# Expert stage of a hybrid decoder layer: token rows gathered as quarter rows and turned by VectorE in 32x32 blocks instead of by TensorE

## The reference

```python
order = jnp.argsort(flat_e)                       # flat_e: expert of each (token, choice) pair, 4096 of them
padded = ((counts + 127) // 128) * 128            # each expert's rows padded to blocks of 128
rows = jnp.zeros((n_rows, 1024)).at[dest].set(h[stok])          # token rows, gathered by expert

def expert_block(args):                           # xb 128 x 1024, e the expert of the block
    xb, e = args
    hid = jax.nn.silu(xb @ w_gate[e]) * (xb @ w_up[e])          # 1024 x 512 each
    return hid @ w_down[e]                                      # 512 x 1024

out = lax.map(expert_block, (rows.reshape(n_blocks, 128, -1), block_e))
return segment_sum(out[dest] * gate, stok)        # added to x, then a last RMSNorm
```

## Time and profile before

| | us |
|---|---|
| median of 3 runs | 2213.04 (2211.13 to 2219.3) |
| the profiled execution | 2212.72 |
| its span | 2211.1 |
| expert loop, first gate product of the loop to the last | about 1261 to 2138 |
| PE busy | 1996.7 (90%) |
| DVE busy | 1415.3 (64%) |
| ACT busy | 1072.4 (49%) |
| POOL busy | 525.4 (24%) |

### The profile page before, as it was taken

The page is one execution under the profiler, slowest core; times in us unless marked ns, Lnnn a source line. Parts: engine busy times, 40 slices in busy tenths (PEclk is TensorE's granted clock), DMA queues, the critical chain, the costliest instruction groups (busy, mean ns, idle before and its releaser), DMA issues. The chain is left out here.

```text
span 2211.1 us, 32053 instructions
## 1 busy us (share of the span) xinstructions
PE 1996.7 (90%) x10153; PEld 1672.5 (76%) x10154; DVE 1415.3 (64%) x2368; ACT 1072.4 (49%) x1591; POOL 525.4 (24%) x637
## 2 busy tenths in 40 slices
PE   6999999886898988969996699999999999999970
PEld 5887888785687878858885588888888888888860
DVE  4675687466797887945556675675568755546344
ACT  4322211224377787753223364665567655545433
POOL 2000111241000000000000254454445545344430
PEclk9999999998899999989997699999999999999995
DMA  8675986835435323024335588797889978667637
GB/s 263 218 228 196 327 288 223 262 133 124 123 69 125 76 69 67 1 84 167 134 134 200 196 309 281 255 331 273 283 277 387 348 268 304 188 229 238 218 85 314
DMA packets 170121, 458.37 MB, mean 207 GB/s; under 512 B 19872, under 2 KB 69104, under 8 KB 144432
## 3 DMA queue, kind: packets, MB, share of 16 engines
q1 hardware_dynamic: 122896, 285.30, 37.4%
q0 software_dynamic: 31008, 138.37, 20.5%
q10 hardware_dynamic: 16128, 33.56, 4.3%
HBM read 342.08 MB, written 115.10 MB: 207 GB/s over the span
## 5 line engine op out<-in xcount | busy, mean ns | idle before, releaser
L2215 DVE TENSOR_TENSOR w_down_lo<-w_down_raw,w_down_hi 128x2048 fp32r<-128x2048 f32 x64 | 144.1, 2289 | 124.5 <-ACT w_down_hi L2152 123.0
L2299 PE MATMUL m_bank<-w_down_hi,hidden_T_hi 128*128 128x512 f32 x392 | 160.4, 409 | 6.8 <-DVE w_down_lo L2215 6.8
L2215 DVE TENSOR_TENSOR w_gate_lo<-w_gate_raw,w_gate_hi 128x2048 fp32r<-128x2048 f32 x63 | 141.6, 2289 | 38.8 <-ACT w_gate_hi L2152 32.4
L2278 PE MATMUL m_bank<-w_gate_hi,rows_T_hi 128*128 128x512 f32 x392 | 156.5, 399 | 6.4 <-DVE rows_T_lo L2220 3.9
L2278 PE MATMUL m_bank<-w_up_hi,rows_T_hi 128*128 128x512 f32 x392 | 158.8, 405 | 0.0
L2279 PE MATMUL m_bank<-w_gate_lo,rows_T_hi 128*128 128x512 f32 x392 | 156.1, 398 | 0.0
L2280 PE MATMUL m_bank<-w_gate_hi,rows_T_lo 128*128 128x512 f32 x392 | 156.0, 398 | 0.0
L2215 DVE TENSOR_TENSOR w_up_lo<-w_up_raw,w_up_hi 128x2048 fp32r<-128x2048 f32 x64 | 146.2, 2287 | 15.1 <-ACT w_up_hi L2152 15.1
L2300 PE MATMUL m_bank<-w_down_lo,hidden_T_hi 128*128 128x512 f32 x392 | 155.4, 396 | 0.0
L2280 PE MATMUL m_bank<-w_up_hi,rows_T_lo 128*128 128x512 f32 x392 | 154.8, 395 | 0.0
L2279 PE MATMUL m_bank<-w_up_lo,rows_T_hi 128*128 128x512 f32 x392 | 154.5, 394 | 0.0
(11 more groups left out here) (424 smaller groups left out, 5288.3 us busy)
## 6 DMA issues: line engine op xcount, KB each, us to landing
w_gate_raw<-in_w_gate_dram SPq DMA_DIRECT2D x64, 1024.0 KB
w_down_raw<-in_w_down_dram POOLq DMA_DIRECT2D x64, 1024.0 KB
w_up_raw<-in_w_up_dram SPq DMA_DIRECT2D x64, 1024.0 KB, 8.2
hT_d<-hT_parts SPq DMA_DIRECT2D x32, 512.0 KB, 5.2
hT_parts<-hT_d SPq DMA_DIRECT2D x32, 512.0 KB, 9.0
k_parts<-kT_d SPq DMA_DIRECT2D x64, 256.0 KB, 8.5
u_tok<-in_x_dram SPq DMA_DIRECT2D x16, 512.0 KB, 5.8
qT_d<-qk_out ACTq DMA_DIRECT2D x32, 256.0 KB, 3.8
```

Source lines behind the costliest of these rows:

```text
L2215: dve.tensor_tensor(wlo[w][:, halves[i]], raw[w][:, halves[i]], whi[w][:, halves[i]], ALU.subtract).then_inc(lo_done[w], 1)
L2278: pe.matmul(to[:], xh[:, k], whi[w][:, c], start=k == 0, stop=False)
L2299: pe.matmul(DN[h][:], hh[:, k], whi[2][:, part(k)], start=k == 0, stop=False)
```

## The change

**Gather.** The row gather inside the loop becomes four indirect DMAs (`gather_parts`). DMA r fetches 128 quarter rows of 256 floats into columns 256r to 256r+255 of `x`: partition 32f+i gets quarter f of the row of slot 32r+i. The first two blocks are still gathered and turned in the old way.

**Turn.** PE's eight transposes leave the loop. DVE turns the rows with two instructions of 32x32 block transposes (`turn`), 128x512 each, that read `x` at every eighth float and write a new SBUF tile `xT` in contiguous runs of 32. They stand at the head of each DVE iteration, behind a wait for the four DMAs (`x_in`) and for DVE's own last `rows_lo`, and ahead of `hidden_lo`. `rows_hi` and `rows_lo` of the loop read `xT` instead of PSUM; `rows_hi` now also waits for `u_done`, which the turned rows in PSUM implied before.

**Indices.** The row numbers of the quarters (4 x row + quarter) are made once, on DVE and PE, in `part_rows`: a 128x512 copy, four small copies or shifts, four 128x64 matmuls on PE behind the first gate product, and one scaling. DVE also copies each block's columns of indices (`part_index`, `slot_index`), which POOL did before; for that it waits until the last addition of rows (`out_st`) and the last gate gather (`gate_in`) have landed. POOL keeps one small add ahead of its indirect DMAs (`pause`), none ahead of the gate gather.

The diff, cut to its core:

```diff
+    def gather_parts(self, pool, d):
+        for r in range(PARTS):
+            pool.indirect_dma_start(self.x[:, r * PART:(r + 1) * PART], None, d["h2"].rearrange("r (f c) -> (r f) c", f=PARTS),
+                                    bass.IndirectOffsetOnAxis(ap=self.part_idx[:, r:r + 1], axis=0)).then_inc(self.x_in, 16)
...
             @block.gpsimd
...
                 with pool.Fori(0, later(pool) - 1) as j:
                     past, now = place(pool, j), place(pool, j + 1)
                     e = expert(pool, now + 1)
-                    pool.wait_ge(xT_psum, 2 * j + 6)
-                    gather(j + 3)
-                    add_rows(j, j + 1, 2 * j + 4)
-                    gather_gate(j + 1, j + 2)
+                    pool.wait_ge(store.pauses, 2 * j + 2)
+                    pool.wait_ge(turned, 2 * j + 2)
+                    pool.wait_ge(part_ready, j + 2)
+                    store.pause(pool, ones)
+                    store.gather_parts(pool, d)
+                    add_rows(2 * j + 3, 2 * j + 4, 2 * j + 3)
+                    gather_gate()
...
             @block.vector
...
+                def turn(h):
+                    dve.transpose(xT[:, 4 * h:4 * h + 4].rearrange("p k (r i) -> p r k i", r=PARTS),
+                                  x[:].rearrange("p (r j k) -> p r k j", r=PARTS, k=KT)[:, :, 4 * h:4 * h + 4]).then_inc(turned, 1)
...
                 first_rows_lo(1, 2)
                 split_lo(1, 0, 1)
+                part_rows()
                 split_lo(2, 0, 0)
...
                 with dve.Fori(0, later(dve)) as j:
                     before, now, order = place(dve, j), place(dve, j + 1), place(dve, j + 2)
+                    dve.wait_ge(x_in, 64 * j + 96)
+                    dve.wait_ge(xl_done, 2 * j + 4)
+                    turn(0)
+                    turn(1)
+                    part_index(j + 3)
                     hidden_lo(j + 2)
...
                     hidden(j + 1)
                     rows_lo(0, 2 * j + 5)
                     rows_lo(1, 2 * j + 6)
+                    dve.wait_ge(out_st, 16 * j + 16)
+                    slot_index(j, True)
+                    dve.wait_ge(gate_in, 16 * j + 16)
+                    slot_index(j + 1, False)
...
             @block.tensor
...
                 product(G, 0, g_done)
+                pe.wait_ge(pick_set, 2)
+                for r in range(PARTS):
+                    last = pe.matmul(PI[:, r * NBLK:(r + 1) * NBLK], pick[:, r].rearrange("p f i -> p (f i)"), ids_f[:], start=True, stop=True)
+                last.then_inc(part_psum, 1)
...
                     product(U, 1, u_done)
-                    pe.wait_ge(x_in, 16 * j + 48)
-                    rows_T(0)
-                    rows_T(1)
                     down(j, before)
```

More of the change, by code:

```diff
@@ L43 @@
 NBLK = 64
+PARTS = 4
+PART = D // PARTS
+QUAD = P // PARTS
 MIN_BLK = 2 * SEQ // P
@@ L2063, in experts @@
         sem = ctx.enter_context(phase_semaphores(nc))
-        bank = [ctx.enter_context(nc.psum_tensor(f"m_bank{i}", [P, BANK], F32)) for i in range(7)]
-        G, U, XT, HT, DN = bank[0], bank[1], bank[2:4], bank[4], bank[5:7]
+        bank = [ctx.enter_context(nc.psum_tensor(f"m_bank{i}", [P, BANK], F32)) for i in range(8)]
+        G, U, XT, HT, DN, PI = bank[0], bank[1], bank[2:4], bank[4], bank[5:7], bank[7]
         FT = FF // P
@@ L2216, in split_lo, with first_rows_lo @@
                                       ALU.subtract).then_inc(lo_done[w], 1)
-                def rows_lo(h, want):
+                def first_rows_lo(h, want):
                     dve.wait_ge(xh_done, want)
@@ L2221, in rows_lo, with part_rows, part_index, slot_index @@
                                       ALU.subtract).then_inc(xl_done, 1)
+                def rows_lo(h, want):
+                    dve.wait_ge(xh_done, want)
+                    dve.tensor_tensor(xl[:, 4 * h:4 * h + 4], xT[:, 4 * h:4 * h + 4], xh[:, 4 * h:4 * h + 4],
+                                      ALU.subtract).then_inc(xl_done, 1)
+                def turn(h):
+                    dve.transpose(xT[:, 4 * h:4 * h + 4].rearrange("p k (r i) -> p r k i", r=PARTS),
+                                  x[:].rearrange("p (r j k) -> p r k j", r=PARTS, k=KT)[:, :, 4 * h:4 * h + 4]).then_inc(turned, 1)
+                def part_rows():
+                    dve.memset(part_ids[:, NBLK * PARTS:], 0)
+                    dve.tensor_copy(pick[:], ident[:].rearrange("p (r o i) -> p r o i", r=PARTS, o=1).to_broadcast([P, PARTS, PARTS, QUAD])).then_inc(pick_set, 1)
+                    dve.tensor_copy(ids_f[:], ids[:, 0:NBLK]).then_inc(pick_set, 1)
+                    dve.tensor_copy(quad_i[:], const.tok[:, 0:1]).then_inc(pick_set, 1)
+                    dve.wait_ge(pick_set, 3)
+                    dve.tensor_scalar(quad_i[:], quad_i[:], 5, None, ALU.logical_shift_right).then_inc(pick_set, 1)
+                    dve.wait_ge(pick_set, 4)
+                    dve.tensor_copy(quad[:], quad_i[:]).then_inc(pick_set, 1)
+                    dve.wait_ge(pick_set, 5)
+                    dve.wait_ge(part_psum, 1)
+                    dve.tensor_scalar(part_ids[:, 0:NBLK * PARTS].rearrange("p (b r) -> p b r", r=PARTS), PI[:, 0:PARTS * NBLK].rearrange("p (r b) -> p b r", r=PARTS),
+                                      float(PARTS), quad[:, 0:1], ALU.mult, ALU.add).then_inc(part_set, 1)
+                    dve.wait_ge(part_set, 1)
+                    part_index(2)
+                def part_index(b):
+                    dve.tensor_copy(store.part_idx[:], part_ids[:, bass.ds(b * PARTS, PARTS)]).then_inc(part_ready, 1)
+                def slot_index(b, of_rows):
+                    if of_rows:
+                        dve.tensor_copy(to_idx[:], ids[:, bass.ds(b, 1)]).then_inc(slot_ready, 1)
+                    else:
+                        dve.tensor_copy(gate_idx[:], gate_ids[:, bass.ds(b, 1)]).then_inc(slot_ready, 1)
                 def hidden(b):
@@ L2243, in _ @@
                 hidden(0)
-                rows_lo(0, 3)
-                rows_lo(1, 4)
+                first_rows_lo(0, 3)
+                first_rows_lo(1, 4)
                 with where_below(nc, dve, first, second):
@@ L2264, in _ @@
                 end = later(dve)
+                dve.wait_ge(out_st, 16 * end + 16)
+                slot_index(end, True)
                 hidden_lo(end + 2)
```

73 lines of the change are left out of this document (42 added, 31 removed).

## The result

The changed kernel takes 2239.4 us (median of 4 runs, 2235.5 to 2245.9) against 2214.0 us before, a ratio of 1.0109 with a 95% interval of 1.0092 to 1.0126. It is slower by 25 us, where 29 us less had been forecast. The profiled execution has a span of 2233.9 us.

A forecast was written before the change was run, and what follows sets the result against it. PE was taken to bound the kernel, with DMA setting the long runs of new blocks. 2212.7 - 42.7 (transposes) + 12 (long runs) + 2.5 (ahead of the loop) - 0.3 (index copy) = 2184.2 us; range 2168 to 2215.

The forecast's parts named there:

- PE, removed: Expert loop: eight transposes leave PE, 0.89 us per iteration, 42.7 us over 48; an iteration takes 17.26 instead of 18.15 us.
- DVE, added: Head of each DVE iteration: two turns at 1.1 us each, 2.35 us with a small copy; two index copies, 0.3 us.
- the fourth rival: Turn on DVE itself slow: beyond 1.5 us each its slack is gone; at 2.2 us each, 2243 us; chance 0.11.
- DMA and DVE in the long runs: Consecutive new blocks in the loop: DMA needs 19.5 us per block against PE's 17.26, DVE lag beside it; +12 us.
- the run of seven: Loop's seven consecutive new blocks, whose weights must be loaded and split; forecast to lose 9 us after 6.5 us is absorbed.
- the 0.5 us a block that quarters were to cost the DMA engines: Row gather in the loop: 512 pieces of 1 KB instead of 128 of 4 KB, 0.5 us more; bounds nothing and 1.7.
- Ahead of the loop: `part_rows` before DVE's first down split waits for PE, delaying splits and the loop's first gate product: +2.5 us (0 to 4).
- Behind the loop: After the loop's last gate product: transposes gone, 0.89 us per iteration; index copy gone at the last addition of rows, -0.3 us.
- POOL and the queues: POOL in the loop: four gathers cost 4 x 1.03 us, land before the next turn; no wait expected, cost nothing.
- The third rival: Head of DVE: turn waits for four gathers landing over 4.2 us behind down loads; 14 us, 2195 us; chance 0.10.

The follow-up runs named there:

- one gather: Changed kernel with one gather of 128 whole rows in place of four of quarter rows, turn kept (rows turned wrongly): 2185.0 us, ratio 0.9855.
- PSUM splits: First kernel of the experiments: changed kernel whose lo splits in the loop subtract a PSUM tile instead of the SBUF hi part (wrong result): 2186.0 us, ratio 0.9858.
- fourth: Changed kernel with the two turns moved behind hidden_lo and the gate split: 2232.7 us, ratio 1.0073.
- fifth kernels: Changed kernel where DVE, in the loop, waits for its own previous lo split to end before issuing the next: 2212.3 us, ratio 0.9978.
- two tiles: Changed kernel with two tiles for gathered rows, used in turn, quarters asked for one iteration earlier: 2222.0 us; with waits between lo splits added, 2228.6 us.

## Why the prediction was wrong, point by point

- **PE, removed: right.** Where repeat blocks follow each other in the kernel after, gate products start at 1894.88, 1912.10, 1929.33 and 1946.56: 17.23 us, forecast 17.26, before 18.15.
- **DVE, added: right within 0.1 us a turn.** 1.20 us for 1.1; the index copies 0.12 to 0.19. The slow turn, the fourth rival, didn't come. Some of this is luck: the copy that gave 1.1 us reads PSUM in one run and steps by eight floats where it writes, while the turn steps where it reads.
- **DMA and DVE in the long runs: near, a little too high.** With one gather the run of seven shows iterations of 17.9, 18.9, 19.5 and 18.8 us, and the loop loses 822.2 - (854.9 - 41.8) = 9.1 us in all, 7.5 with the PSUM splits; forecast 12. That DMA sets these iterations was not tested by a run of its own, and the 0.5 us a block that quarters were to cost the DMA engines doesn't show: the kernel with quarters and PSUM splits loses less than the one with whole rows.
- **Ahead of the loop: too small.** Forecast +2.5 (0 to 4), measured +5.5. Of this 0.9 us are not the stage's: its first gate product begins at 1245.03 in place of 1244.13. From there to the loop it is 21.2 us in place of 16.5, so +4.6 (the fourth and fifth kernels of the experiments, with the same code there, have 19.7 and 19.8, so +3.2 and +3.3). DVE waited for the four small matmuls until 1254.62 in place of 1251.5, so the down and gate splits came that much later. Timeline of DVE after:

```profile
1254.62 0.49 DVE L2263 TENSOR_SCALAR part_ids<-m_bank,quad 128x256 int32<-128x256 f32 x1 [6.61 <-PE m_bank L2384]
```

- **Behind the loop: small.** From its last gate product to the end the kernel after is 2.7 us shorter. The forecast has 0.89 (the last transposes) and 0.3 (the index copy) there; the rest isn't traced.
- **POOL and the queues: wrong, and this is the step that failed.** "Four gathers cost 4 x 1.03 us ... No wait expected." They took 4.7 to 17.0 us a block. The loop lost 874.8 - 813.1 = 61.7 us where 12 was forecast for everything; with gathers of 1.0 us, or with one, it lost 7.5 to 9.1. The other 53 come from the held gathers. The 1.03 us came from a gather at 1294.62, and at 1294.66 DVE began `rows_T_lo`, which then read PSUM. It was the price of a place where nothing holds POOL. The rows to be read were next to it: the addition of rows took 3.72 us beside the down splits, and the same instruction takes 1.60 us in the kernel before where DVE is idle:

```profile
2135.46 1.60 POOL L2117 DMA_INDIRECT x_d<-rows_out,to_idx  x1 [0.28 <-issue]
```

- **The third rival named the wait, and sized it a quarter.** "The turn waits for the four gathers at the head, and all splits queue behind it" is what happened. It was priced at 14 us and made to depend on landing behind the down loads. It depended on the length of the round from one turn over four gathers to the next: free where the gathers take 5 us, and longer than the iteration where they take 17. In the runs of new blocks iterations of 20 to 22 us follow each other, and also single new blocks reach 20.

The Trainium skill has the rule under "SBUF — State Buffer", section "Who interferes with whom": a DVE instruction with two SBUF inputs contends with a GpSimd instruction that reads SBUF, over ports that the two engines share and that one of them holds exclusively. The first and fifth kernels agree with it: 1.00 us without the second input, and none over 3.1 us once the splits have gaps. The same section has it that the form with two inputs did not stall DMAs; here the measurement decides for the indirect ones, which were held for up to 8.6 us, while the plain loads that POOL issues in the loop of the kernel after never took over 0.66. That a hold can outlast one split is seen only in these runs. I had read the page for the step of eight floats and not for the neighbour on POOL.

## What to carry to other kernels

Price an instruction by a row in which its neighbours do what they will do at the new place; a GpSimd instruction above all, beside DVE instructions with two SBUF inputs. Before multiplying a DMA issue by four, ask how long each can be held, and whether the next round of them waits for what this one delivers: such a round must fit into an iteration with the holds in it. Where many such DVE instructions follow each other, a short wait between them can be worth more than it costs: 27 us in the changed kernel, though beside two tiles it made things 6.6 us slower.

## What the runs showed of the hardware

- A quarter gather of 128 pieces of 1 KB takes POOL 0.95 us beside an idle DVE and 1.9 us where it is held by one split of 2.3 us. Where it stays held through a row of splits back to back it takes 4.2 to 5.1 us for two and 8.6 for four; 23 of 56 gathers in the kernel after were let in earlier, behind the first split, and took 1.9 to 2.9 us. The small `paused` instruction on POOL is held as well, up to 7.5 us beside four splits in the kernel with one gather. Whether the gather is of quarters or of whole rows doesn't matter (0.94 to 1.02 us against 1.02, unheld).
- A wait costs PE more than its own length. After 2.46 us of idling PE began its gate product at 1434.54; the granted clock was 1.00 in the first microsecond, 0.76 in the next and 0.50 (1.2 of 2.4 GHz) in the two after it, with matmuls of 0.63 us for 0.40. Windows of the kernel after, in the columns of the earlier trace rows:

```profile
1434.00:1435.00 1.00, 0.46 (x2) 0.45 (x3) 1.00 (x4) 1.00 (x2) 1.00 (x1) 1.00 1.02 426
1435.00:1436.00 1.00, 1.00 (x6) 0.77 (x5) 1.00 (x1) 1.00 (x1) 0.69 (x2) 0.76 1.06 422
1436.00:1438.00 2.00, 2.00 (x6) 1.62 (x5) 2.00 (x2) 0.41 (x1) 2.00 (x1) 0.50 1.13 404
```

Over the loop PE was busy 832.5 us for the work that took it 816.7 with one gather. That is 16 us on top of 42 of idling, and a forecast of waits has to add it. The clock is about half of it: behind the first iteration the loop has six stretches at 0.50, some 20 us together, so some 10 us lost (an estimate from these stretches), against one such stretch with one gather. The rest is not explained by any row.
